# Two transformer blocks in one kernel: the path for overfull experts moved into the expert loop, expert sums added to the last product in PSUM, and the second block's projection begun with its values

## What is computed

```python
    y = lax.map(expert_block, (blk_e, row_tok.reshape(n_blocks, MOE_BLOCK), row_w.reshape(n_blocks, MOE_BLOCK)))
    out = jax.ops.segment_sum(y.reshape(R, D), row_tok, num_segments=T)
    ...
        x = x + g2 * sparse_moe(h, ...)
    ...
        xn = _rms(x, norm_w[l])
        h = jnp.einsum('bsd,de->bse', xn, w_in[l])
        qa, ka, va, ga, qr, kr, vr, gr = jnp.split(h, offsets, axis=-1)
```

## Time and profile before

| | |
|---|---|
| median of 3 runs | 1942.26 us (1942.21 to 1946.23) |
| profiled execution, own time | 1944.41 us |
| span in the trace | 1942.4 us |
| PE, DVE, ACT, POOL busy | 1810.5, 695.7, 337.0, 139.2 us |
| expert loop | about 495 to 1540 us of the span |
| seam, last expert's end to the first projection | 1540.22 to 1576.53 us |
| attention's projection | 1576.53 to 1699.13 us |

### The profile page before, as it was taken

One profiled execution on the slowest core, in us unless ns is written; L12 is line 12 of the kernel. 1 busy time (PEld: TensorE's weight loads), 2 busy tenths in 40 slices (PEclk: granted clock), 3 DMA queues, 4 the chain that ended last, 5 costly groups with the idle time before them and its releaser, 6 DMA issues.

```text
span 1942.4 us, 31934 instructions
## 1 busy us (share of the span) xinstructions
PE 1810.5 (93%) x13194; PEld 844.9 (43%) x13194; DVE 695.7 (36%) x1750; ACT 337.0 (17%) x724; POOL 139.2 (7%) x208
## 2 busy tenths in 40 slices
PE   4999999997999999999999998999999679989989
PEld 2466746744433332333233332333333235856754
DVE  3368956504322222232222221231313254095140
ACT  2226711612001000000000000000000022061010
POOL 1020000000011111001111111011101000000000
PEclk9999999999899999999999999999999989999999
DMA  9722331422699999999999999999999681100001
GB/s 321 222 83 88 95 101 44 174 92 92 250 376 400 392 405 404 402 395 401 400 402 401 400 402 407 400 386 392 405 402 412 217 281 65 44 1 1 0 1 44
DMA packets 133402, 495.25 MB, mean 255 GB/s; under 512 B 22587, under 2 KB 72677, under 8 KB 84104
## 3 DMA queue, kind: packets, MB, share of 16 engines
q1 hardware_dynamic: 116048, 464.81, 61.3%
q0 software_dynamic: 11264, 19.27, 4.2%
q10 hardware_dynamic: 5944, 9.09, 1.3%
HBM read 481.08 MB, written 17.43 MB: 257 GB/s over the span
## 4 chain that ended last, share of the span: by engine, by line
PE 68%; DMA 20%; DVE 7%; SPq 2%; issue 2%; ACT 1%; ACTq 0%; DVEq 0%
PE bank L1472 20%; DMA ring<-in_exp_w_dram 19%; PE bank L415 10%; PE bank L1495 10%; PE bank L425 8%; PE bank L827 6%; PE bank L608 2%; SPq L928 1%; PE bank L798 1%; DVE arena L689 1%; PE bank L586 1%; DVE arena L774 1%; PE bank L597 1%; PE bank L391 1%; DMA arena<-in_x_dram 1%
## 5 line engine op out<-in xcount | busy, mean ns | idle before, releaser
L1472 PE MATMUL bank<-ring,arena 128*32 128x512 f32 x5568 | 635.7, 597 | 28.7 <-DMA ring<-in_exp_w_dram 25.3
L1472 PEld LDWEIGHTS bank<-ring,arena 128*32 128x32 f32 x5568 | 170.2, 110 | 379.1 <-issue 322.9
L1495 PE MATMUL bank<-ring,arena 128*32 128x512 f32 (+1 forms) x3392 | 309.9, 519 | 18.2 <-DMA ring<-in_exp_w_dram 16.9
L415 PE MATMUL bank<-hT,ring 128*128 128x512 f32 x448 | 207.5, 615 | 9.5 <-DVE hT L804 7.5
L1495 PEld LDWEIGHTS bank<-ring,arena 128*32 128x32 f32 x3392 | 110.1, 110 | 221.2 <-issue 175.7
L425 PE MATMUL bank<-ring,hT 128*128 128x256 f32 (+1 forms) x768 | 156.4, 363 | 0.0
L425 PEld LDWEIGHTS bank<-ring,hT 128*128 128x128 f32 x768 | 135.5, 190 | 18.4 <-issue 2.4
L415 PEld LDWEIGHTS bank<-hT,ring 128*128 128x128 f32 x448 | 86.5, 197 | 113.8 <-issue 110.4
L1889 DVE COPY arena<-bank 128x8 f32<-128x8 f32 (+1 forms) x32 | 5.3, 165 | 361.5 <-PE bank L1445 351.5
L1204 ACT ACTIVATE arena<-bank 128x384 f32<-128x384 f32 (+2 forms) x64 | 29.5, 460 | 573.0 <-PE bank L1460 572.9
L1903 DVE TENSOR_TENSOR arena<-bank,arena 128x512 f32<-128x512 f32 x87 | 54.9, 684 | 188.2 <-PE bank L1472 188.2
(11 more groups left out here) (359 smaller groups left out, 1525.4 us busy)
## 6 DMA issues: line engine op xcount, KB each, us to landing
ring<-in_exp_w_dram SPq DMA_DIRECT2D x384, 1024.0 KB, 27.4
ring<-in_ada_w_dram SPq DMA_DIRECT2D x24, 1024.0 KB, 10.2
ring<-in_w_in_dram SPq DMA_DIRECT2D x23, 1024.0 KB, 10.1
ring<-in_w_out_dram SPq DMA_DIRECT2D x8, 1024.0 KB, 5.1
arena<-in_x_dram ACTq DMA_DIRECT2D x1, 2048.0 KB, 17.8
ring<-in_w_in_dram SPq DMA_DIRECT2D x8, 256.0 KB, 5.5
expert_sums<-arena POOLq DMA_DIRECT2D x4, 512.0 KB, 4.2
h_rows<-arena ACTq DMA_DIRECT2D x4, 512.0 KB, 3.3
```

Source lines behind the costliest of these rows:

```text
L415: mm = pe.matmul(z[:, :], w, hT[:, k, :], start=(k == 0), stop=(k == ND - 1))
L1472: mm = pe.matmul(bank[g][QUAD * c:QUAD * (c + 1), :].rearrange("p (h n) -> p h n", h=2), rowsT[:, k, QUAD * g:QUAD * (g + 1)], w[:, :, SW ...
L1495: mm = pe.matmul(bank[b][QUAD * c:QUAD * (c + 1), 0:width], actT[:, g, 2 * q + j, :], w[:, col:col + width], start=(q == 0 and j == 0), st ...
```

## The change

1. The general path of every engine is now a function, called inside the expert loop after iteration `GENERAL_AT` = 19 (SP: at the top of its iteration 20). It has row, index and result buffers of its own (`over_...`).
2. DVE's eight additions of the last expert (L1993) are gone. The last product leaves its banks open (`stop=False`), and PE adds `y_rows` to it, by matmuls with the identity in place of the transposes; DVE adds each bank to `resT` once.
3. The loads of `y_rows` are issued by SP, ahead of the second block's weights, when the sums of the last expert but one have landed. SP no longer waits for the general path or for `y_rows` before it loads weights.
4. `da_jobs` begins with the four jobs for the values. They read `h_raw`, which is `resT` times the norm's weights without the root (ACT), and DVE multiplies their results by the root of each token ("root").
5. The sums of squares are taken after the first of these jobs, in four groups of 32 columns of PE, folded to one number a token in the middle of the second job (`token_sums`), and the root is spread over partitions after it (`roots_in_rows`, four matmuls). DVE writes `hT` for the other jobs after that.
6. The ring's order of the second block's weights follows: parts 4 and 5 (the values) come first.

The core of the diff (the first `general_path()` is SP's, the second stands in the loops of PE, DVE, ACT and POOL):

```diff
+GENERAL_AT = 19
-    after = [("w_in_2", i, 1) for i in range(14)] + [("w_out_2", i, 1) for i in range(4)]
+    after = [("w_in_2", i, 1) for i in (4, 5, 0, 1, 2, 3, *range(6, 14))] + [("w_out_2", i, 1) for i in range(4)]
...
+        da_values = [v_job("w_in_2", 4 + c, 0, SW, 2 * i, vtok[:, 2 * i:2 * i + 2, SW * c:SW * c + SW], "root")
+                     for c in range(2) for i in range(2)]
+        da_jobs = da_values + da_jobs
...
+                elif j["how"] == "root":
+                    dve.wait_ge(z_done, j["at"] + 1)
+                    root = row_root[:, j["i0"]:j["i0"] + 2].unsqueeze(2).to_broadcast([P, 2, SW])
+                    ins = dve.tensor_tensor(j["dst"], job_z(j), root, ALU.mult)
...
+                if n == GENERAL_AT + 1:
+                    general_path()
...
-            sp.wait_ge(over_done, 1)
+            sp.wait_ge(w1_used, 8 * NEXP)
+            sp.wait_ge(main.at_ok, NEXP)
+            sp.wait_ge(main.free, NEXP - 1)
             for i in range(NT):
-                sp.wait_ge(y_in[i], 16)
+                sp.dma_start(y_rows[i], y_dram[P * i:P * (i + 1), :]).then_inc(y_in[i], 16)
             for name, part, m in AFTER:
                 load(name, part, PLACE[name, part], m)
...
+                if n == GENERAL_AT:
+                    general_path()
...
             act.preload_act_table_set("natural_log_exp_and_others")
-            act_norm(act, link, 2)
-
+            for t in range(ND):
+                act.wait_ge(res_ok, ND + t + 1)
+                act.activation(h_raw[:, t, :], resT[:, t, :], ACT.Copy, scale=vecs[:, 64 + t:65 + t]).then_inc(hs_ok, 1)
+            for t in range(ND):
+                if t >= 4:
+                    act.wait_ge(sum_ok, 2 * ND + t - 3)
+                act.activation(sq4[t % 4], resT[:, t, :], ACT.Square).then_inc(sq_ok, 1)
...
+            act.wait_ge(sum_ok, 3 * ND)
+            act.activation(sq_part, bank[5][:, :], ACT.Copy).then_inc(part_ok, 1)
+            act.wait_ge(sum_ok, 3 * ND + 1)
+            link(act.activation(row_root, bank[6][:, 0:NT], ACT.Ln, scale=1.0 / (32 * D), bias=eps))
+            act.activation(row_root, row_root, ACT.Exp, scale=-0.5).then_inc(rstd_ok, 1)
...
             for t in range(4):
                 for h in range(2):
                     rows = slice(HD * h, HD * (h + 1))
-                    mm = pe.matmul(bank[4 * h + t][:, :], y_last[rows, P * t:P * (t + 1)], hot_last[rows, :], start=True,
-                                   stop=True)
-                mm.then_inc(last_t, 1)
-            pe.wait_ge(last_ok, ND)
+                    pe.matmul(bank[4 * h + t][:, :], y_last[rows, P * t:P * (t + 1)], hot_last[rows, :], start=True,
+                              stop=False, skip_group_check=True)
             for i in range(NT):
                 pe.wait_ge(y_in[i], 16)
+            for t in range(ND):
+                for i in range(NT):
+                    mm = pe.matmul(bank[t][:, i * P:(i + 1) * P], y_rows[i][:, P * t:P * (t + 1)], ident[:, :], start=False,
+                                   stop=(i == NT - 1), skip_group_check=True)
+                mm.then_inc(y_used, 1)
+            def square_sums():
                 for t in range(ND):
-                    mm = pe.transpose(bank[t][:, i * P:(i + 1) * P], y_rows[i][:, P * t:P * (t + 1)], ident[:, :])
-                mm.then_inc(y_used, 1)
-            pe.wait_ge(res_ok, ND + 1)
-            pe_norm(pe, 2)
-            pe_project(pe, da_jobs, 2 * ND)
+                    c = t % 4
+                    pe.wait_ge(sq_ok, 2 * ND + t + 1)
+                    pe.matmul(bank[5][QUAD * c:QUAD * (c + 1), :], ones[:, 0:QUAD], sq4[c], start=(t < 4), stop=(t >= 4))\
+                      .then_inc(sum_ok, 1)
...
+            v0, v1 = da_values[0]["at"], da_values[1]["at"]
+            pe_project(pe, da_jobs, 2 * ND, {v0: square_sums, v1: roots_in_rows}, {v1: token_sums})
...
-            dve.wait_ge(b2_ok, ND)
-            for j in range(4):
-                dve.wait_ge(last_t, j + 1)
-                for t in (j, 4 + j):
-                    dve.scalar_tensor_tensor(out=resT[:, t, :], in0=bank[t][:, :], scalar=mod[:, 40 + t:41 + t],
-                                             in1=resT[:, t, :], op0=ALU.mult, op1=ALU.add).then_inc(last_ok, 1)
-            dve.wait_ge(y_used, NT)
             for t in range(ND):
+                dve.wait_ge(y_used, t + 1)
                 dve.scalar_tensor_tensor(out=resT[:, t, :], in0=bank[t][:, :], scalar=mod[:, 40 + t:41 + t],
                                          in1=resT[:, t, :], op0=ALU.mult, op1=ALU.add).then_inc(res_ok, 1)
...
-            dve_norm(dve, link, 2, vecs[:, 64:72], h_ok)
             dve.wait_ge(dist_ok, 3)
...
+            dve.wait_ge(rstd_ok, 3)
...
+            def normed():
+                dve.wait_ge(sum_ok, 3 * ND + 2)
+                for t in range(ND):
+                    dve.scalar_tensor_tensor(out=hT[:, t, :], in0=resT[:, t, :], scalar=vecs[:, 64 + t:65 + t],
+                                             in1=bank[3][:, :], op0=ALU.mult, op1=ALU.mult).then_inc(h_ok, 1)
+            dve_project(dve, link, da_jobs, {da_values[1]["at"]: normed})
```

More of the change, by code:

```diff
@@ L401, in pe_project @@
             waiting, folding = [], []
+            first = next(j for j in jobs if j["kind"] == "T")
             for j in jobs:
@@ new lines, in token_sums, with roots_in_rows @@
+            def token_sums():
+                pe.wait_ge(part_ok, 1)
+                for i in range(NT):
+                    mm = pe.matmul(bank[6][:, i:i + 1], sq_part[:, i * P:(i + 1) * P], ones[:, 0:1], start=True, stop=True)
+                mm.then_inc(sum_ok, 1)
+            def roots_in_rows():
+                pe.wait_ge(rstd_ok, 4)
+                for i in range(NT):
+                    mm = pe.matmul(bank[3][:, i * P:(i + 1) * P], row_root[:, i:i + 1].to_broadcast([P, P]), ident[:, :],
+                                   start=True, stop=True)
+                mm.then_inc(sum_ok, 1)
```

277 lines of the change are left out of this document (157 added, 120 removed).

## The result

The median went from 1942.77 us (1942.21 to 1946.23, 4 runs) to **1928.77 us** (1925.23 to 1930.95, 4 runs). The ratio is 0.9922, with a 95% interval of 0.9903 to 0.9942. 1929.4 us was predicted, from 1923.5 to 1936. The same kernel, timed again in a later batch, took 1929.75 us against 1942.17 for before. The profiled execution of the changed kernel took 1927.72 us, with a span of 1925.5.

A forecast was written before the change was run, and what follows sets the result against it. The expert loop was taken as bound by weight transfers from HBM, PE close behind, PE being the bound in the projection. Terms: -17.0 - 2.8 + 6.3 + 0.6 = -12.9 us, giving a median of 1929.4 us, range 1923.5 to 1936.

The forecast's parts named there:

- The seam: Between last expert and projection: the first values job starts 17.0 us earlier, at 1559.5 in place of 1576.53.
- the first rival: At the seam: `y_rows` land near 1545.5 on SP's queue and the clock doesn't fall, 2.8 + 2.0 us more; chance 0.15.
- The half clock at the projection's start: At the projection's start: the 2.8 us lost to half clock from 1576.53 on are gone.
- 6.3 us of added work: On PE in the projection: sums of squares 4.2 us, token sums 1.1, spreading the root 1.0.
- The root hidden: Beside the values jobs: the root is ready near R + 17.8 (R: DVE's last addition), wanted at R + 20.2; 2 us cover.
- the second rival: In the projection: values jobs wait for the root, PE waits at `roots_in_rows`; 1933 us; chance 0.09.
- The general path in the loop: Behind expert 19's iteration: the jump stalls PE at least 4.84 us, mostly hidden; priced between 0 and 5 us, taken as 0.6.
- the third rival: In the loop: the jump's stall is up to 10 us under load, 3 to 8 us stay, 1932 to 1937 us; chance 0.19.
- a sign of error: At the loop's end: last expert ends within 1 us of 1540.2 if right; moving by more than 2 us means wrong.
- Part 3: At the seam: SP issues the `y_rows` loads earlier, moving them 1.4 us forward, the last landing at about 1548.3.

The follow-up runs named there:

- experiment 2: Changed kernel with the general path called after expert 30 in place of 19 (`GENERAL_AT = 30`): 1931.55 us.
- experiment 4: Changed kernel with parts 4 to 6 undone (old norm ahead of all projections, old order of jobs and weights), parts 1 to 3 kept: 1935.25 us.
- experiment 1: Changed kernel with the general path left out of every engine's program, so nothing jumps anywhere: 1928.54 us.
- experiment 3: Changed kernel with the general path called four times, behind experts 17, 18, 19 and 20: 1932.35 us.
- experiment 6: Changed kernel with ACT issuing the four `y_rows` loads without waiting for `y_last`, and SP waiting for them before the weights: 1925.53 us.
- experiment 7: Changed kernel with each load of `y_rows` added by PE to all banks as it lands, in place of bank by bank: 1928.22 us.
- experiment 10: Changed kernel with the first `y_rows` load added to all banks when it lands, the other three bank by bank: 1925.73 us.

## Why the prediction was right

- **The seam, 17.0 us predicted.** 16.8 and 17.2 us in two profiled executions. Its parts held too: PE idle ahead of the products 3.07 and 3.88 us (3.5), products 10.21 and 8.91 us (9.6), 1.69 us from there to the first job (1.55). That they agree so closely is in part luck. The prediction took it that the clock falls in PE's wait. In experiment 2, with the same code at the seam, it held, and the first job came after 16.8 us, so that the seam gave 19.4. The 2.0 us that the first rival adds for a clock that doesn't fall are real (2.8 measured), and the prediction could not know which would come.
- **The half clock at the projection's start, 2.8 us, and 6.3 us of added work**, net +3.5. The projection took 3.4 us longer. The sums of squares took 1565.62 - 1561.25 = 4.4 us (4.2), the fold 0.8 (1.1), the spreading 1.0 (1.0). The seam and the projection together: -13.5 predicted, -13.3 and -13.8 in the two traces.
- **The root hidden.** The cover was put at 2 us and was 1.8. PE did not wait at L1679, which decided against the second rival. Experiment 4 puts this part and its price together: with the root ahead of the projection again the stretch is 6.1 to 8.8 us longer.
- **The general path in the loop, 0.6 us.** Experiment 1 puts it at 0.2 to 1.2, which can't be told from nothing, so that 0.6 itself is not shown; 3 us or more, as in the third rival, is not borne out. The reason given, that the queue is longer than the stall and that PE has waits to catch up in, is shown by experiment 3. One thing is missing in the prediction and in the rival: the clock falls in the loop as well, 2.4 us more. It too is paid from PE's waits: the transposes of hidden rows that stood at 1136.73, 1168.88 and 1203.17 us stand at 1132.14, 1169.85 and 1198.51, which is 4.6 us ahead, 1.0 behind, and again 4.7 ahead. The delay lived for one expert. The stall did not grow with busy DMA engines, as the page of the Trainium skill made one fear (Runtime: NRT & Kernel Launch, section Instruction fetch mechanics, by which the fetch is a DMA): 4.2 to 5.4 us in six places of the loop (at one of them with 2.1 us more behind it), 4.84 in the seam. The rival's 10 us under load were wrong. The trace has the fetches of instructions as a DMA queue of its own (q8), with one packet in some 14 us of the loop. In the seam's gap and in each of the six of the loop one such packet starts, 1.5 to 2.8 us after PE's last matmul. That agrees with the page, though the packets don't say which engine they are for.
- **What was off.** The last expert was to end within 1 us of 1540.2, and a move of 2 us was named a sign of error. It ended at 1534.67, and in other runs between 1534.8 and 1540.7. This isn't the change: the first transpose of hidden rows already stands between 522.0 and 526.3 us in runs whose code is the same up to there, and the loop varies by 3 us (1011.2 to 1014.3 with the jump at expert 19). As a test of the change this sign was useless; a stretch that starts at an event inside the kernel was the right one.
- **Part 3** was given 1.4 us for loads issued earlier. The size was right and the cause only in part: against `y_last` the first load is issued 1.5 us earlier than before (0.52 us ahead, and 1.01 behind). By experiment 6 only 0.5 us of this are SP's queue. The other 1.0 us comes without it, when ACT no longer reads the number of blocks and branches between `y_last` and its loads, and that is part 1. From the first issue to the first product, which waits for all four loads, there are 8.1 and 8.9 us on SP's queue and 8.5 on ACT's, so the first rival, by which the queue was the cause and the loads would land 3 us sooner on another, fell. The 7.9 us that the prediction gives there for the old loads are 8.4 by its own rows (1541.28 to 1549.7), which changes nothing.

## What to carry to other kernels

A stall in a stretch that waits for transfers anyway costs nearly nothing as long as it is shorter than what is queued and is followed by enough waits to be repaid. At a seam it costs what it sticks out over the next thing waited for. Here that was less than its 4.84 us: the last load of `y_rows` landed at 1549.7 and PE went on at 1552.55, so the stall by itself is worth some 2.9 us there, an estimate from the earlier trace rows, and it becomes worth more only when the loads come earlier. When a chain on the path is shortened, look at what PE does in the gaps that remain: gaps of 3 to 5 us cost nothing in two profiles and 1.5 to 3 us of low clock in the others, and work that must be done anyway (here a quarter of the products) is best put there. Let two engines go bank by bank at the same rate; when all banks become complete only at the end, the second engine's whole time lies on the path.

## What was not expected of the hardware

- The clock over a gap of 3 to 4 us is not decided by its length: it held over 3.24 us (experiment 2) and 3.31 us (experiment 4), with products of 7.38 us, and fell over 3.07 (the changed kernel), 3.64 (experiment 1) and 3.88 us (the changed kernel again), with products of 10.21, 8.96 and 8.91 us. The instructions of PE ahead of the gap are the same in all five.
- At the attention's start the same code shows the low clock in some profiled executions and not in others. In the changed kernel it fell where PE had idle pieces of 1.26 and 1.55 us among short work, and eight records of L749 took 1.91 us and not 1.06; in experiment 7 the clock held over the same two pieces:

```profile
1689.50 1.11 PE L740 MATMUL bank<-ident,arena 128*128 128x128 f32 x4 [0.71 <-DVE arena L789]
1690.40 1.91 PE L749 MATMUL bank<-arena 128*128 128x128 f32 x8
1692.25 2.08 PE L732 MATMUL bank<-arena 64*128 64x512 f32 x4
```

  Twenty microseconds on, the changed kernel is 2.2 us behind experiment 7. A second such place is the start of the retention. In experiment 10 its 16 records of L1709 took 9.74 us where the same work took 7.30 in the changed kernel (L1705), and the next 32 records 6.24 and not 3.84. Its rest from the first scores on is the longest, 245.9 us, against 243.9 in the changed kernel and 240.1 in experiment 4. So code that no edit touched differs by up to 5.8 us between profiles, more than most experiments here were to show; what decides it stays open.
